# Grouped attention rebuilt on high and low halves: stacked queries, undivided weights, division per head at the end

## The reference

```python
def gqa_sdpa(q, k, v):
    B, Q, H, Dh = q.shape
    qg = q.reshape(B, Q, N_KV_HEADS, KV_GROUP, Dh)
    s = jnp.einsum("bqkgd,bskd->bkgqs", qg, k).astype(jnp.float32) * (Dh ** -0.5)
    p = jax.nn.softmax(s, axis=-1).astype(v.dtype)
    o = jnp.einsum("bkgqs,bskd->bqkgd", p, v)
    return o.reshape(B, Q, H * Dh)

qx = apply_rope(rmsnorm((hx @ wq).reshape(B, S, N_HEADS, HEAD_DIM), q_g), cos, sin)
kx = apply_rope(rmsnorm((hx @ wk).reshape(B, S, N_KV_HEADS, HEAD_DIM), k_g), cos, sin)
k_all = jnp.concatenate([kx, kc], axis=1)        # kc, vc: the same of the context
v_all = jnp.concatenate([vx, vc], axis=1)
yx = gqa_sdpa(qx, k_all, v_all) @ wo             # in query blocks of 128
```

## Time and profile before

| | us |
|---|---|
| median of 3 runs | 3809.29 (3808.97 to 3809.36) |
| profiled execution, span | 3805.8 |
| input stage, from its first weights' low half to the first scores | 2972 to 3083.9 |
| attention loop and its tail, to the first output product | 3083.9 to 3335.2 |
| PE busy, whole span | 3497.2 (92%) |
| DVE busy | 2273.1 (60%) |
| ACT busy | 1557.0 (41%) |

### The profile page before, as it was taken

The page is one execution under the profiler, slowest core; times in us unless marked ns, Lnnn a source line. Parts: engine busy times, 40 slices in busy tenths (PEclk is TensorE's granted clock), DMA queues, the critical chain, the costliest instruction groups (busy, mean ns, idle before and its releaser), DMA issues.

```text
span 3805.8 us, 41708 instructions
## 1 busy us (share of the span) xinstructions
PE 3497.2 (92%) x15968; PEld 2700.7 (71%) x15968; DVE 2273.1 (60%) x3115; ACT 1557.0 (41%) x2242; POOL 981.4 (26%) x793
## 2 busy tenths in 40 slices
PE   5989999999989998999789997699999989999998
PEld 4757778886757776777659964357887656668886
DVE  5664556564857779495967669854233765443233
ACT  3653233333643233233554464354222654442222
POOL 4404546653404544454412015400000000000000
PEclk9989999999989999999899998799999989999999
DMA  5403534543303434344228721013332100013332
GB/s 198 123 23 108 155 125 152 176 151 87 107 12 111 149 117 122 116 121 131 76 66 258 217 69 45 28 45 89 99 93 73 56 23 1 1 50 98 102 89 67
DMA packets 552732, 373.69 MB, mean 98 GB/s; under 512 B 28862, under 2 KB 526872, under 8 KB 551509
## 3 DMA queue, kind: packets, MB, share of 16 engines
q1 hardware_dynamic: 522928, 278.19, 25.3%
q0 software_dynamic: 29408, 92.76, 7.4%
q10 hardware_dynamic: 196, 0.07, 0.0%
HBM read 368.85 MB, written 2.10 MB: 97 GB/s over the span
## 4 chain that ended last, share of the span: by engine, by line
PE 69%; DVE 21%; ACT 5%; issue 4%; DMA 1%; SPq 0%; DVEq 0%; POOL 0%; ACTq 0%
PE PS L375 18%; PE PS L377 18%; PE PS L376 18%; DVE mod_acc L1052 4%; DVE CV L1198 3%; PE PS L423 3%; PE PS L848 2%; DVE tmp L1198 2%; PE PS L828 2%; PE PS L838 1%; DVE Wl L1008 1%; DVE cv L1513 1%; DVE stat_r L1079 1%; PE PS L719 1%; ACT L1616 1%
## 5 line engine op out<-in xcount | busy, mean ns | idle before, releaser
L375 PE MATMUL PS<-Hh,Wh 128*128 128x512 f32 (+1 forms) x2816 | 1068.0, 379 | 98.8 <-DVE Wl L1008 62.0
L377 PE MATMUL PS<-Hh,Wl 128*128 128x512 f32 (+1 forms) x2816 | 1045.2, 371 | 0.0
L376 PE MATMUL PS<-Hl,Wh 128*128 128x512 f32 (+1 forms) x2816 | 1045.0, 371 | 0.0
L1979 POOL TENSOR_TENSOR Wl<-raw,Wh 128x1024 fp32r<-128x1024 f32 (+2 forms) x254 | 580.9, 2288 | 740.5 <-ACT Wh L1595 738.8
L375 PEld LDWEIGHTS PS<-Hh,Wh 128*128 128x128 f32 x2816 | 540.9, 192 | 223.3 <-issue 135.7
L1595 ACT ACTIVATE Wh<-raw 128x1024 fp32r<-128x1024 f32 (+2 forms) x558 | 541.1, 971 | 315.7 <-PE PS L377 285.2
L1008 DVE TENSOR_TENSOR Wl<-raw,Wh 128x1024 fp32r<-128x1024 f32 (+2 forms) x304 | 351.0, 1155 | 437.2 <-ACT Wh L1595 436.8
L376 PEld LDWEIGHTS PS<-Hl,Wh 128*128 128x128 f32 x2816 | 541.3, 192 | 91.7 <-issue 6.0
L377 PEld LDWEIGHTS PS<-Hh,Wl 128*128 128x128 f32 x2816 | 540.0, 192 | 90.0
L1052 DVE SCALAR_TENSOR_TENSOR mod_acc<-mod_w,cact,mod_acc 128x256 f32<-128x256 f32 (+1 forms) x644 | 546.1, 890 | 92.4 <-DMA mod_w<-in_w_ada 74.6
L375 PE MATMUL PS<-g_h,Wh 128*128 128x512 f32 (+1 forms) x880 | 337.2, 383 | 15.8 <-DVE g_l L1133 12.5
(11 more groups left out here) (282 smaller groups left out, 4427.1 us busy)
## 6 DMA issues: line engine op xcount, KB each, us to landing
raw<-in_ffn_w SPq DMA_DIRECT2D x132, 512.0 KB, 3.9
mod_w<-in_w_mod POOLq DMA_DIRECT2D x192, 256.0 KB, 3.8
raw<-in_w_up SPq DMA_DIRECT2D x88, 512.0 KB, 4.6
mod_w<-in_w_ada POOLq DMA_DIRECT2D x160, 256.0 KB, 3.9
raw<-in_w_in SPq DMA_DIRECT2D x62, 512.0 KB, 4.5
raw<-in_conv_w_pw SPq DMA_DIRECT2D x48, 512.0 KB, 3.9
raw<-in_ffn_w SPq DMA_DIRECT2D x48, 384.0 KB, 3.4
raw<-in_ffn_w SPq DMA_DIRECT2D x48, 320.0 KB, 3.1
```

The costliest lines, as they stand in the source:

```text
L375: pe.matmul(o, wh, xh, start=start, stop=False, skip_group_check=True)
L376: pe.matmul(o, wh, xl, start=False, stop=False, skip_group_check=True)
L377: return pe.matmul(o, wl, xh, start=False, stop=stop, skip_group_check=True)
L1979: pool.tensor_tensor(low, src, high.bitcast(F32), ALU.subtract).then_inc(*mark("w_low_pool", one[0]))
```

## The change

The layout of the grouped attention is replaced. Every operand is split in halves, and each product has 128 rows:

- **Queries and scores.** `q_parts` holds for each of the 16 heads a 128-row tile: 64 rows of high half and 64 of low half. `k_hi` and `k_lo` hold the doubled keys. Scores are q_parts x k_hi plus q_parts x k_lo: four fp32r matmuls a tile (two of 512 and two of 256 columns) for two float32 ones. That is also the fourth product, low x low.
- **Softmax weights.** ACT's exponential has no row sum any more, and the reciprocal and the scaling of a tile's rows are gone. PE transposes the undivided weights. ACT copies them out as a high half (`pt2_hi`), DVE subtracts it from PSUM for the low half (`pt2_lo`, 128x768).
- **Values.** `v_hi` and `v_lo` have six blocks of 64 columns, the four value heads and two blocks of ones (zeros in `v_lo`), so that a pair of blocks is one value head beside ones. `pv(u)` serves two tiles at once: 18 matmuls of 256 columns (six key blocks, three products), and half of its output rows are the sums of the weights. The result has a bank for each head.
- **Division per head.** After a head's four tiles DVE takes the reciprocal of the 64x512 sums and multiplies the 64x512 result by it into `y_full`; after two heads ACT and DVE split `y_full` into `y2_h` and `y2_l`, which now lie in `q_parts`.
- **Input stage.** Queries and keys pass through four buffers `heads_in`; `high_parts` (ACT) and `low_parts` (DVE) move them into the split layout in pass i, for job i-3: one instruction each for a key, two of 64 rows each for a query pair. Evicting job i waits until job i-4's buffer is free. Values are split from PSUM. POOL fills the ones and splits the context's keys and values.

The order of the passes changes in the loop: PE issues scores(n), then in odd passes `pv` for the tiles n-5 and n-4, then transposes(n-2).

```diff
         def gqa_attend():
...
+                q, b = q_parts[:, h, i * P:(i + 1) * P], bank_of[job]
+                for k in (k_hi, k_lo):
+                    pe.matmul(PS[:, b, :], q, k[:, g, 0:SEQ], start=k is k_hi, stop=k is k_lo, skip_group_check=True)
+                    mm = pe.matmul(PS[:, b + 1, 0:CTX], q, k[:, g, SEQ:], start=k is k_hi, stop=k is k_lo,
+                                   skip_group_check=True)
...
+                for kb in range(KT):
+                    vh, vl = (v[:, kb, b0:b0 + 2, :].rearrange("p b d -> p (b d)") for v in (v_hi, v_lo))
+                    ph, pl = pt2_hi[u % 2][:, kb, :], pt2_lo[u % 2][:, kb, :]
+                    pe.matmul(o, vh, ph, start=kb == 0, stop=False, skip_group_check=True)
+                    pe.matmul(o, vh, pl, start=False, stop=False, skip_group_check=True)
+                    mm = pe.matmul(o, vl, ph, start=False, stop=kb == KT - 1, skip_group_check=True)
...
+            for n in range(len(tiles) + 5):
                 if n < len(tiles):
                     scores(*tiles[n])
-                if 0 <= n - 3 < len(tiles):
-                    pv(n - 3, *tiles[n - 3])
+                if n >= 5 and n % 2 == 1:
+                    pv((n - 5) // 2)
                 if 0 <= n - 2 < len(tiles):
                     turn(n - 2, *tiles[n - 2])
```

DVE, in the input stage and in the loop:

```diff
+                if s == "x" and i >= 3 and jobs[i - 3][0] != "v2":
+                    low_parts(jobs[i - 3])
...
+            dve.wait_ge(*ready("high_parts", job))
+            if name == "k2":
+                i = dve.tensor_tensor(k_lo[:, g, 0:SEQ], src[:, :], k_hi[:, g, 0:SEQ].bitcast(F32), ALU.subtract)
+            else:
+                for e in range(2):
+                    at_h, at_l = slice(e * HD, (e + 1) * HD), slice((1 - e) * HD, (2 - e) * HD)
+                    i = dve.tensor_tensor(q_parts[at_l, 2 * g + e, :], src[at_h, :],
+                                          q_parts[at_h, 2 * g + e, :].bitcast(F32), ALU.subtract)
...
-            if 0 <= n - 1 < len(tiles):
-                dve.wait_ge(*free(("s2", *tiles[n - 1])))
-                t = own(dve.reciprocal(ri[(n - 1) % 3], rs[(n - 1) % 3]))
+            if 0 <= n - 2 < len(tiles):
+                job, u = ("pt2", *tiles[n - 2]), (n - 2) // 2
+                cols = slice((n - 2) % 2 * P, ((n - 2) % 2 + 1) * P)
+                dve.wait_ge(*ready("pt2_high", n - 2))
+                dve.tensor_tensor(pt2_lo[u % 2][:, :, cols], banks2(job, KT * P).rearrange("p (k c) -> p k c", c=P),
+                                  pt2_hi[u % 2][:, :, cols].bitcast(F32), ALU.subtract).then_inc(*empty(job))
+            if n >= 8 and n % QT == 0:
...
+                t = own(dve.reciprocal(y_part[at_y, :], bank(job)[at_sum, :]))
                 dve.wait_ge(*t)
-                p = p2[(n - 1) % 3][:, :]
-                dve.tensor_scalar(p, p, ri[(n - 1) % 3], None, ALU.mult).then_inc(*mark("p2_scaled", *tiles[n - 1]))
...
+                dve.tensor_tensor(y_full[h % 2 * HD:(h % 2 + 1) * HD, 0:SEQ], bank(job)[at_y, :], y_part[at_y, :],
+                                  ALU.mult).then_inc(*empty(job))
```

ACT, in the input stage and in the loop:

```diff
+                    if s == "x":
+                        o = head_in(job)[:, :]
+                        if i >= len(heads_in):
+                            act.wait_ge(*head_in_free(jobs[i - len(heads_in)]))
...
+                if s == "x" and i >= 3 and jobs[i - 3][0] != "v2":
+                    high_parts(jobs[i - 3])
...
-                act.activation(p2[n % 3][:, :], banks2(job, W), ACT.Exp, bias=nm[n % 3], scale=scale,
-                               accum_out=rs[n % 3]).then_inc(*empty(job))
+                act.activation(p2[n % 3][:, :], banks2(job, SEQ + CTX), ACT.Exp, bias=nm[n % 3], scale=scale)\
+                   .then_inc(*empty(job))
             if 0 <= n - 2 < len(tiles):
...
+                act.activation(pt2_hi[u % 2][:, :, cols], banks2(job, KT * P).rearrange("p (k c) -> p k c", c=P), ACT.Copy)\
+                   .then_inc(*mark("pt2_high", n - 2))
```

More of the change, by code:

```diff
@@ L325, in attention_jobs, with head_in, head_in_free @@
         return jobs + [("q2", s, j) for j in range(KD)] if s == "x" else jobs
+    def head_in(job):
+        return heads_in[attention_jobs("x").index(job) % len(heads_in)]
+    def head_in_free(job):
+        return full(("turned", *job)) if job[0] == "v2" else ready("low_parts", job)
     WARM = 8
@@ L604, in attention_inputs @@
                     pe.wait_ge(*ready("head_scaled", *jobs[two]))
[L605 removed]
+                    pe.matmul(bank(job), const("swap_pair"), head_in(jobs[two])[:, :],
                               start=True, stop=True).then_inc(*fill(job))
@@ L834, in turn @@
                 begin(job, "pair")
-                pe.wait_ge(*ready("p2_scaled", h, i))
-                for kb in range(kt):
+                pe.wait_ge(*free(("s2", h, i)))
+                for kb in range(KT):
                     c = slice(kb * P, (kb + 1) * P)
-                    mm = pe.transpose(banks2(job, kt * P)[:, c], p2[n % 3][:, c], const("ident"))
+                    mm = pe.transpose(banks2(job, KT * P)[:, c], p2[n % 3][:, c], const("ident"))
                 mm.then_inc(*fill(job))
[L841 to L853, removed]
@@ L1274, in attention_inputs @@
             jobs = attention_jobs(s)
-            for i in range(len(jobs) + 2):
+            for i in range(len(jobs) + 3):
                 if i < len(jobs):
@@ L1544, in _ @@
         scale = float(HD) ** -0.5
-        for n in range(len(tiles) + 5):
+        for n in range(len(tiles) + 6):
             if n < len(tiles):
@@ L1730, in attention_inputs @@
             jobs = attention_jobs(s)
-            for i in range(len(jobs) + 1):
+            for i in range(len(jobs) + (3 if s == "x" else 0)):
                 if i < len(jobs):
@@ L1739, in attention_inputs, with high_parts @@
                         square(job, o, n)
-                if s == "x" and i >= 1 and jobs[i - 1][0] != "v2":
-                    root(("ss", *jobs[i - 1]), n)
+                if s == "x" and 1 <= i <= len(jobs):
+                    if jobs[i - 1][0] != "v2":
+                        root(("ss", *jobs[i - 1]), n)
+                    else:
+                        c = jobs[i - 1][-1]
+                        turned = ("turned", *jobs[i - 1])
+                        act.wait_ge(*full(turned))
+                        act.activation(v_hi[:, 0:QT, 3 * c:3 * c + 3:2, :],
+                                       bank(turned, n).rearrange("p (t g d) -> p t g d", t=QT, g=2), ACT.Copy)\
+                           .then_inc(*mark("v_high", c))
+                if s == "x" and i >= 3 and jobs[i - 3][0] != "v2":
+                    high_parts(jobs[i - 3])
+        def high_parts(job):
+            name, _, g = job
+            src = head_in(job)
+            act.wait_ge(*ready("rotated", ("swap2", name, g)))
+            if name == "k2":
+                i = act.activation(k_hi[:, g, 0:SEQ], src[:, :], ACT.Copy)
+            else:
+                for e in range(2):
+                    i = act.activation(q_parts[e * HD:(e + 1) * HD, 2 * g + e, :], src[e * HD:(e + 1) * HD, :], ACT.Copy)
+            i.then_inc(*mark("high_parts", job))
         for i, (o, src) in enumerate(pieces[0]):
@@ L1917, in _ @@
         scale = float(HD) ** -0.5
-        W = SEQ + CTX
-        for n in range(len(tiles) + 5):
+        for n in range(len(tiles) + 6):
             if n < len(tiles):
```

125 lines of the change are left out of this document (87 added, 38 removed).

## The result

| | us |
|---|---|
| median after, 4 runs | 3896.19 (3895.67 to 3899.08) |
| median before, 4 runs | 3809.13 (3804.18 to 3809.36) |
| ratio | 1.0239, 95% interval 1.0227 to 1.0251 |
| profiled execution after | 3894.3, before 3805.8 |

The direction and the range held; the effect, forecast at 37 us, is 87 by the medians. The two profiled executions lie 88.5 us apart. Cut into the same four stretches, they differ by

A forecast was written before the change was run, and what follows sets the result against it. PE limits the loop before; after the change the DVE and ACT ring was to bound it. Profiled 3805.8 + 18 (loop) + 19 (input stage) = 3842.8, median 3.5 above: 3846 us, range 3833 to 3911.

The forecast's parts named there:

- the division's term: Loop, DVE: reciprocal and product enter the ring every fourth tile, 1.34 us a head; 14 divisions make 18.8 us.
- Rival B: Division on DVE: the reciprocal doesn't stream, 7 ns an element, 3.73 us each; total 3893 us; chance 0.35.
- A: Whole kernel: the forecast as summed, with a streaming reciprocal, 3846 us, own range 3836 to 3857; chance 0.50.
- the Trainium skill's rule: Division on DVE: eight streaming steps an element would give 4.45 us a division, total near 3904; identified with Rival B.
- The ring: Loop, DVE and ACT: maximum, negative, exponential, high half, low half close a circle once a tile, 3.69 us.
- the prediction's loop: First maximum to last low half: rings, divisions, y_l and tail sum to 265.6 us against 247.5, +18.
- The clock: Loop, PE: 2 us allowed for a beginning at half clock, which the ring mostly covers.
- rival C: Loop: PE stays at 1.2 GHz and decides, 5.18 us a tile, total 3926 us; chance 0.04.
- The input stage: Evictions wait for low parts four jobs earlier; tied query evictions 11.42 us apart; +19 us in all.
- POOL: Ahead of the input stage: its ten instructions lie hidden under the normalization; uncovered they would cost some 10 us.
- D: Loop: the ring isn't closed because ACT or DVE overlap, PE bounds at the limit, total 3763 us; chance 0.05.
- E: Input stage: it hides its ties, total 3827 us; chance 0.04.

The follow-up runs named there:

- experiment 3: Changed kernel with ACT's high half of tile n-2 moved ahead of tile n's exponential, division left whole: 3861.0 us, ratio 1.0142 to the kernel before.
- 1: Changed kernel with DVE's 64x512 reciprocal replaced by a plain copy, so the output is not the reference's: 3857.6 us, ratio 1.0133 to the kernel before.
- experiment 2: Changed kernel with each head's division cut into four 64x128 pieces, one a pass ahead of the low half: 3834.9 us, ratio 1.0075 to the kernel before.
- experiment 6: Changed kernel with PE making every tile's scores twice, result unchanged: 3908.2 us, ratio 1.0265 to the kernel before.
- experiment 4: Changed kernel with six input-stage buffers for queries and keys in place of four: 3877.5 us, ratio 1.0182 to the kernel before.
- experiment 5: Changed kernel with division in four pieces, high half ahead of the exponential, and six input buffers together: 3791.8 us, ratio 0.9959 to the kernel before.
- 7: As experiment 5, but ACT copies results and sums out of PSUM and one reciprocal serves two heads: 3772.8 us, ratio 0.9912 to the kernel before.

## Why the prediction was right in sign and wrong in size

**The step that failed is the price of the reciprocal in the division's term.** It took the reciprocal of 64x512 as streaming, 0.69 us, "as the single element shows no surcharge". It takes 3.355: 2.67 us more in each of 16 heads, 43 us, by far most of the 50 that the forecast was short. The reading, not the arithmetic, was at fault. A row of one element is all fixed part, 153 ns like any other instruction of that length, and cannot tell 1 ns an element from 6. Rival B had the mechanism with 7 ns and 3893 us, within 3 us of the result, and should have been likelier: nothing in the trace excluded it. That it came so near is in part luck: its 7 ns, a middle between two bounds, was 0.75 too much, some 6 us in 16 heads, against pieces elsewhere that were too small. The stated range held the result because it reached into B; A's own, 3836 to 3857, did not. (Its lower end, 3833, is 3 us below A's own, and no term gives these 3.) Of the Trainium skill's rule ("VectorE: DVE Perf Modes", section "First, the fixed hardware budget": an iterative divide with repeat count 8) the direction is right, an element does cost several steps; by the two sizes it is 6.25 / 1.05 = 6.0 streaming steps here, not 8, so the estimate of 4.45 us was 1.1 too long and its 3904 us 8 too many.

**The ring is right.** 3.69 us predicted, 3.69 measured; opening it (3) or removing what stands in it (1, 2) gives time back, and 45 us of work on PE (6) cost 13. With the reciprocal's true length the prediction's loop would be 265.6 + 42.7 = 308.3, measured 309.2. Within that, a division's handovers were 0.2 us too short (the reciprocal starts 0.99 behind the low half, the maximum 0.73 behind the product, where 0.88 and 0.61 were taken); against that the part behind the last maximum, without the surplus of its two reciprocals, was 1.1 us too long in the sum.

**The clock: the size came out, by luck, and the reason did not.** The allowance was 2 us for a beginning at half clock. Four stretched passes show 2.1 (4.23, 4.73, 3.79 and 4.11 in place of 3.68, with a granted clock of 0.74 to 0.94 in them), but they lie in the middle and at the end of the loop; the beginning lost nothing. Against rival C the prediction held that the clock is 1.00 in the whole loop of before; that didn't carry over, it was 0.83. The closed ring hid it: C's conclusion, that PE sets the pace, was wrong all the same. The clock surfaced in experiments 3 and 6, as soon as PE was needed again.

**The input stage is right in its mechanism,** 19 predicted, 21.5 measured. Tied evictions are 11.62 apart for 11.42: the first low part starts 0.72 behind the rotation's last row, not 0.61, and the two with the step to ACT take 1.42, not 1.34. But experiment 4 takes away only 16.6 where the ties had been summed to 18.9, and leaves 4.8 where the rest had been put at 0: two errors that partly cancel.

**POOL was not quite hidden.** Four rows of DVE beside it are longer than before, by 1.0 us together (the last section).

**C, D and E** are out: PE at a lower clock did not set the pace, the ring is closed, the ties show.

## What to carry to other kernels

Of an operation known only from a row of one element, the trace gives the fixed part and nothing else; price the element from a second size, or keep the whole range likely. The reciprocal cost by its row's length here, not by its rows: stack two heads in 128 partitions, cut it in pieces, and put them where the engine waits already. Before replacing PE work by work on DVE and ACT, draw the circle that the program's order makes of them. Here two blocks in the other order on ACT, the division in a wait and two more buffers turned +2.4% into -0.4%, and pairing the heads made it -0.9%.

## What the runs showed of the hardware

- A reciprocal on DVE costs 6.25 ns an element and 155 ns fixed: 153 ns for 1, 955 for 128, 3355 for 512 columns; 943 for 128 columns in 128 rows.
- PE's clock fell behind long rests. In experiment 3, after 4 us of rest and some 1 us of work it ran at 0.50 for over 3 us; with the rest filled by useless products it stayed at 1.00, and the kernel became 31 us faster for 49 us more work. Work spread evenly over the passes (6) did not do it. How much PE works in all doesn't tell the clock. Between 3130 and 3310, in this order experiments 5, 6 and 2:

```profile
3130.00:3310.00 180.00, 134.45 (x964) 117.31 (x961) 172.50 (x270) 87.42 (x108) 0.00 (x0) 0.99 0.00 1
...
3130.00:3310.00 180.00, 136.47 (x819) 121.94 (x818) 110.52 (x131) 60.96 (x76) 0.00 (x0) 0.86 0.00 1
...
3130.00:3310.00 180.00, 138.65 (x912) 121.35 (x912) 156.38 (x244) 78.97 (x102) 0.00 (x0) 0.93 0.00 1
```

Up to 3290, experiment 6 has eight rests of about 4 us, experiment 5 none above 1.04. But experiment 2 has none above 1.05 either and got 0.93, and the loop of before began with 15.9 us at 0.50 while PE worked without a rest. What sets the clock there, and how long it stays low, no run here settles.

- DVE's rows grow beside POOL. While POOL splits the context's values, a DVE row of 128x512 takes 1.10 us; the same row took 0.69 before the change. After, POOL's row and DVE's, then DVE's of before:

```profile
2963.72 1.05 POOL L2098 TENSOR_TENSOR v_lo<-v_ctx,v_hi 128x256 fp32r<-128x256 f32 x1
2964.22 1.10 DVE L1098 SCALAR_TENSOR_TENSOR stat_r<-stat_t,stat_y 128x512 f32<-128x512 f32 x1
...
2961.59 0.69 DVE L1079 SCALAR_TENSOR_TENSOR stat_r<-stat_t,stat_y 128x512 f32<-128x512 f32 x1
```

It took 1.10 in experiments 3, 4, 5 and 7 too. That the two share something is only inferred from their lying side by side; no run moved POOL's part away.
